# Sixteen dots of gathered rows: all inside the gates turns, or twelve there and four behind the low parts that follow

## The reference

```python
    def block(args):
        xb, idb, gb = args
        a = jnp.einsum('tkd,td->tk', expert_down[idb], xb)
        act = jax.nn.gelu(a.astype(jnp.float32), approximate=False).astype(xb.dtype) * gb
        return jnp.einsum('tk,tkd->td', act, expert_up[idb])
```

## Time and profile before

| what | us |
|---|---|
| median of 3 runs (lowest to highest) | 1464.06 (1463.61 to 1468.02) |
| the profiled execution | 1463.16 |
| its span, first to last instruction | 1461.3 |
| TensorE busy | 1420.1 |
| VectorE busy | 1183.7 |
| ScalarE busy | 667.6 |
| GpSimd busy | 562.5 |

### The profile page before, as it was taken

The page is one execution under the profiler, slowest core; times in us unless marked ns, Lnnn a source line. Parts: engine busy times, 40 slices in busy tenths (PEclk is TensorE's granted clock), DMA queues, the critical chain, the costliest instruction groups (busy, mean ns, idle before and its releaser), DMA issues.

```text
span 1461.3 us, 21875 instructions
## 1 busy us (share of the span) xinstructions
PE 1420.1 (97%) x7662; PEld 1279.3 (88%) x7662; DVE 1183.7 (81%) x2465; ACT 667.6 (46%) x1085; POOL 562.5 (38%) x458
## 2 busy tenths in 40 slices
PE   3999999999999899999999999999999999999998
PEld 3787789999999899999988888888888888888887
DVE  6987975678888888899678787878788888888887
ACT  3566553444445666777533333333333333333334
POOL 0000001264454458888533343433344344344440
PEclk9999999999999999999999999999999999999999
DMA  9965433455554477787899989999999899999994
GB/s 347 387 216 194 160 106 120 129 197 180 172 179 140 147 253 267 272 295 258 332 370 369 369 313 388 340 353 340 334 329 380 316 374 346 343 373 360 318 330 145
DMA packets 187710, 407.03 MB, mean 279 GB/s; under 512 B 13192, under 2 KB 100816, under 8 KB 185936
## 3 DMA queue, kind: packets, MB, share of 16 engines
q1 hardware_dynamic: 148016, 245.96, 48.6%
q0 software_dynamic: 36864, 134.23, 25.0%
q10 hardware_dynamic: 2720, 25.44, 4.7%
HBM read 362.59 MB, written 42.99 MB: 278 GB/s over the span
## 4 chain that ended last, share of the span: by engine, by line
PE 89%; DVE 4%; ACT 2%; SPq 1%; issue 1%; POOL 1%; DMA 1%; DVEq 0%; ACTq 0%; POOLq 0%
PE bank L2069 12%; PE bank L2071 12%; PE bank L2070 12%; PE bank L1996 11%; PE bank L1998 11%; PE bank L1997 11%; PE bank L2051 5%; PE bank L1965 2%; PE bank L1966 2%; PE bank L1964 2%; SPq L536 1%; PE bank L1986 1%; DMA w_in_sb<-in_w_in 1%; DVE part L1231 1%; PE bank L1848 1%
## 5 line engine op out<-in xcount | busy, mean ns | idle before, releaser
L1996 PE MATMUL bank<-h2hi,dhi 128*128 128x384 f32 x1024 | 346.6, 338 | 4.2 <-DVE dlo L1440 4.1
L1998 PE MATMUL bank<-h2hi,dlo 128*128 128x384 f32 x1024 | 343.2, 335 | 0.0
L1997 PE MATMUL bank<-h2lo,dhi 128*128 128x384 f32 x1024 | 342.8, 335 | 0.0
L2069 PE MATMUL bank<-uhi,ahi 128*128 128x512 f32 x768 | 298.8, 389 | 0.0
L2070 PE MATMUL bank<-ulo,ahi 128*128 128x512 f32 x768 | 298.8, 389 | 0.0
L2071 PE MATMUL bank<-uhi,alo 128*128 128x512 f32 x768 | 298.7, 389 | 0.0
L1440 DVE TENSOR_TENSOR dlo<-down,dhi 128x1024 fp32r<-128x1024 f32 x128 | 161.8, 1265 | 159.8 <-ACT dhi L961 159.8
L739 POOL DMA_INDIRECT rows<-in_peer_up,ids x128 | 162.9, 1273 | 236.7 <-DVE y L1524 206.9
L739 POOL DMA_INDIRECT rows<-in_peer_down,ids x128 | 163.2, 1275 | 215.7 <-DVE rows L1515 197.0
L961 ACT ACTIVATE dhi<-down 128x1024 fp32r<-128x1024 f32 x128 | 135.1, 1056 | 206.3 <-PE bank L1998 205.9
L1996 PEld LDWEIGHTS bank<-h2hi,dhi 128*128 128x128 f32 x1024 | 192.4, 188 | 8.9 <-DVE dlo L1440 5.9
(11 more groups left out here) (249 smaller groups left out, 2079.1 us busy)
## 6 DMA issues: line engine op xcount, KB each, us to landing
down<-in_down_t SPq DMA_DIRECT2D x128, 512.0 KB, 5.4
up<-in_peer_up SPq DMA_DIRECT2D x128, 512.0 KB, 7.5
ada<-in_w_ada SPq DMA_DIRECT2D x48, 512.0 KB, 10.4
gate<-gates_dram SPq DMA_DIRECT2D x32, 768.0 KB, 11.9
gates_dram<-stage ACTq DMA_DIRECT2D x11, 2048.0 KB, 7.2
gel_dram<-gel SPq DMA_DIRECT2D x80, 192.0 KB, 3.4
gelu<-gel_dram SPq DMA_DIRECT2D x80, 192.0 KB, 6.5
wq<-in_peer_query SPq DMA_DIRECT2D x16, 512.0 KB, 5.3
```

Source lines behind the costliest of these rows:

```text
L1996: pe.matmul(bank[7 * s][:, 0:TD], dhi[s][:, k, :], h2hi[:, k, 0:TD], start=k == 0, stop=False)
L1997: pe.matmul(bank[7 * s][:, 0:TD], dhi[s][:, k, :], h2lo[:, k, 0:TD], start=False, stop=False)
L1998: last = pe.matmul(bank[7 * s][:, 0:TD], dlo[s][:, k, :], h2hi[:, k, 0:TD], start=False, stop=k == KT - 1)
L2069: pe.matmul(got[:], ahi[j][:, tokens], uhi[j][:, half], start=first, stop=False)
```

## The change

Of the 16 dots that stood in the turns, 12 stay there, spread over the 24 turns by the same formula. The other four are put behind the low parts of down tiles 76, 77, 78 and 79, ahead of the `up_lo` there. The count of dots done before the rounds, and the program from there on, is as it was. GpSimd's program changes through `dots_by_turn` alone.

```diff
-DOTS_HEAD, DOTS_PICKS, DOTS_TURNS = 3, 3, 16
+DOTS_HEAD, DOTS_PICKS, DOTS_TURNS, DOTS_AFTER = 3, 3, 12, 4
 FIRST_DOTS = 3
 DOTS_ROUTING = DOTS_HEAD * (PH - 1 - FIRST_DOTS) + DOTS_PICKS
-DOTS_EARLY = DOTS_ROUTING + DOTS_TURNS
-assert DOTS_TURNS % ROWS_KEPT == 0
+DOTS_EARLY = DOTS_ROUTING + DOTS_TURNS + DOTS_AFTER
+assert DOTS_TURNS % ROWS_KEPT == 0 and DOTS_AFTER % ROWS_KEPT == 0
 ROW_OPS = 2 * PICKS
...
             for n in range(AFTER_G, EARLY + 2):
                 down_lo(n, n % 2)
+                if n - AFTER_G < DOTS_AFTER:
+                    row_op(DOTS_EARLY - DOTS_AFTER + n - AFTER_G)
                 if 2 <= n - AFTER_G < 2 + AHEAD:
                     up_lo(n - AFTER_G - 2)
```

## The result

| | before | with the change |
|---|---|---|
| median of 16 runs | 1463.85 us | 1467.26 us |
| lowest to highest | 1461.93 to 1468.02 | 1465.80 to 1469.23 |
| span of the profiled execution | 1461.3 us | 1466.6 us |

The ratio is 1.0024, with a 95% interval of 1.0017 to 1.0031. The forecast of 1466.0 us and its range of 1462.2 to 1469.5 us hold it. The interval leaves out 1, so the slowdown is clear of the noise, but small.

What follows compares the result with a forecast made beforehand. The prediction took TensorE to bound the kernel. It summed -1.2 us (long turn) and +3.15 us (late gate load) to +1.95 us, so 1465.1 us for the profiled execution and 1466.0 us as median, range 1462.2 to 1469.5 us.

Steps and rivals of the forecast that it cites:

- TensorE sets the end: Whole kernel: TensorE is busy 1420.1 of 1461.3 us, so what it loses, the end loses.
- dots in the turns are free: Gates turns: taking out four dots of 1.21 us only adds VectorE idle time, gain 0.
- The long turn, -1.2 us: Gates turn of 8.92 us, 1.17 too long: turn 5 without its gather relieves GpSimd, gain 1.2 us.
- The rival in which the slow pairs come elsewhere: GpSimd's one-hot pairs cost as before or one turn more: 1467.2 to 1468.4 us, chance 0.08.
- Dots behind the low parts, cost 0: Behind the turns: four dots fit VectorE's waits for ScalarE, low parts stay 4.16 us apart, cost 0.
- x = 4.3 us: Before the rounds: delay of the load of gate tiles 0 to 3 from three more gathers ahead of it.
- eight against five: Gathers between the turns and the gate load: eight (14 to 21) with the change, five (17 to 21) before.
- TensorE loses x - 1.15 = 3.15 us: Rounds' start: gate load delay x less the 1.15 us to spare at the fourth up tile.
- The second, small wait that I expected: TensorE at the rounds' start: about 0.4 us more waiting until the fourth up tile.
- The hidden gate load: Rival before the rounds: gate load delay x stays under 1.15 us, 1462.9 us, chance 0.20.
- the slower case: Rival before the rounds: gate load held longer, x from 6.75 us on, 1470.4 us at x = 8.7, chance 0.14.

## Why the prediction was right, point by point

- **TensorE sets the end; dots in the turns are free.** Right for VectorE's own time: turns of 7.75 us with and without a dot, in every profile with twelve. But a dot was not free for GpSimd's pairs beside it, as the rows above have it.
- **The long turn, -1.2 us.** Right in size in the first comparison, 1.17 us. The reason was half right. TensorE's wait was not half a turn behind turn 5's gather: it ended at 579.09 us, 9.3 us behind the gather's start at 569.80, and between them lie two more slow pairs, of turn 6, that the prediction did not list. Long pairs came in the changed kernel too, in turns 6, 7 and 9. By the rows, what counts is less that turn 5 lost its gather than that the turns behind gathers lost their dots. And I took one profile for the kernel: in its second one the kernel before had two long turns and a late last one, and this gain would have been 3.6 to 4.2 us. That accounts for most of the way from 1.0024 to 0.9995; for 0.9983, where the kernel before has no profile, it is likely but not shown. The rival in which the slow pairs come elsewhere asked this of the changed kernel alone; the long turns came elsewhere in the kernel before.
- **Dots behind the low parts, cost 0.** Right. Low parts 4.16 us apart, and with the late gathers held the moved dots cost nothing at the rounds' start.
- **x = 4.3 us.** Measured 4.48 us (from the low part of tile 81 to the gate's use: 8.19 against 3.71 us). The three gathers were the right ones, the way of counting them was not: eight against five behind the turns is beside the point, since five issued late did the same. The three that run beside the gate load count, and that these are three as well is luck.
- **TensorE loses x - 1.15 = 3.15 us.** It lost 4.43. The wait itself was near what was forecast, 3.0 us by the timeline against 2.7, but the sum had no term for the clock, which stayed at half for about 3 us after the wait and cost 1.44. The second, small wait that I expected did not come, as the slower TensorE no longer reached the late tile first. This is the term that was mis-sized, by 1.3 us where the whole change is 3.4, and that is about the distance of the forecast (1466.0) from the measured 1467.3 us. The range held because it was wide enough for a term that the sum did not have.
- **The hidden gate load and the slower case** did not come. The gathers were not served behind the gate load: they had 87.2% of the engines while it waited, and x was 4.48 us, neither under 1.15 nor over 6.75.

## What to carry to other kernels

When a wait moves later, so do the transfers behind it: ask which load they will run beside, and whether an engine waits for that load, before asking whether the moved work fits. Price a new wait of TensorE of some 3 us at half as much again, for the clock after it; that is what one such wait cost here, and a wait of 1.86 us cost nothing more. And where a term of the sum is a rare late turn seen in one profile, look at what it hangs on before giving it one value; here it decided the sign. The version to keep is one with twelve dots in the turns and the rest in the rounds: 0.9966 and 0.9951 of the kernel before in two sets, and 0.9948 with the gathers in pairs. It was not timed in the first set, where the kernel before took 1463.85 us; against that, its 1463.42 and 1464.09 us would be no gain.

## What the runs showed of the hardware

- A wait of TensorE of 2.5 to 3.3 us was followed by a granted clock of 0.50 for about 3 us (2.82, 2.65 and 2.52 us of waiting in the three profiles of the changed kernel, 3.27 in the one with late gathers), while with matmuls in the gap and 0.56 us of waiting it stayed at 1.00. A wait of 1.86 us, in the run with the gate tile ahead, was not followed by a lower clock in any window of 1 us up to 757 us.
- In 64 of the 148 turns behind a gather GpSimd's first pair of one-hot rows took 2.75 us in place of 1.70, and the second 2.5 to 2.65 us, or 3.6 to 4.8 us when VectorE's dot stood beside it.
- The gate load of 768 KB took 7.1 us from issue to use with its queue alone (6.9 in the run with twelve dots), and 11.3 to 12.1 us beside three gathers of 1.43 us of all engines each.
